# Two mixers: two panel splits moved ahead of the sums and merges in front of them, the branch gates' halves in another order, one dense group ahead of weighted values

## The reference

```python
h = rms_norm(x) * gain + shift                    # modulated by c through w_ada
q, kc, vc, ks, vs, kw, vw, g, mq, mk, mv, branch = split(h @ w_in)
a = nsa_mixer(...)     # compressed, selected and windowed attention, 8 heads, summed by gates
b = moba_mixer(...)    # 8 more heads
gates = sigmoid(branch)                           # two halves of 1024 columns
x = x + gate * ((gates_0 * (a @ w_up_nsa) + gates_1 * (b @ w_up_moba)) @ w_out)
x = x + gate * swiglu(...)                        # the layer's feed-forward part
```

## Time and profile before

| | |
|---|---|
| median of 3 runs | 2084.69 us (2081.43 to 2087.8) |
| the profiled execution | 2091.63 us, its span 2089.8 us |
| busy: PE, PE weight loads | 2009.8 us (96%), 1782.1 us (85%) |
| busy: DVE, ACT, POOL | 1465.0 us (70%), 1090.4 us (52%), 25.7 us (1%) |
| read from HBM | 369.15 MB, 177 GB/s over the span |
| granted PE clock, mean over the span | 0.98 of full |

### The profile page before, as it was taken

How to read it: one execution, slowest core, us unless ns; L and a number is a source line. 1 busy time by engine, 2 the same in 40 slices (tenths; PEclk the granted TensorE clock), 3 DMA queues, 4 the chain that set the end, 5 groups by cost and what they waited for, 6 DMA issues and landing times. The chain is left out here.

```text
span 2089.8 us, 31990 instructions
## 1 busy us (share of the span) xinstructions
PE 2009.8 (96%) x12846; PEld 1782.1 (85%) x12846; DVE 1465.0 (70%) x2323; ACT 1090.4 (52%) x1728; POOL 25.7 (1%) x46
## 2 busy tenths in 40 slices
PE   7899899999899899999999998999999999999999
PEld 4779898888789888899889777898898889898888
DVE  6777678877777577647766767677667757767774
ACT  3545544534545455535554655655545546855552
POOL 1001000000001000000000000000000000000000
PEclk9999999999999999999999999999999999999999
DMA  9445448876445357555556432455555554244554
GB/s 316 160 171 198 159 156 279 276 247 215 140 168 187 110 187 230 189 182 182 189 184 208 145 101 101 141 183 183 185 188 190 181 182 152 73 142 142 181 179 144
DMA packets 266211, 372.28 MB, mean 178 GB/s; under 512 B 8400, under 2 KB 160336, under 8 KB 266064
## 3 DMA queue, kind: packets, MB, share of 16 engines
q1 hardware_dynamic: 264736, 368.97, 53.0%
q10 hardware_dynamic: 1328, 1.26, 0.2%
HBM read 369.15 MB, written 1.05 MB: 177 GB/s over the span
## 5 line engine op out<-in xcount | busy, mean ns | idle before, releaser
L2222 DVE TENSOR_TENSOR parts<-ring,parts 128x2048 fp32r<-128x2048 f32 (+2 forms) x304 | 675.5, 2223 | 376.9 <-ACT parts L703 376.4
L703 ACT ACTIVATE parts<-ring 128x2048 fp32r<-128x2048 f32 (+2 forms) x304 | 565.6, 1861 | 592.8 <-PE psum L1470 323.7
L1470 PE MATMUL psum<-h,parts 128*128 128x512 f32 x1920 | 675.1, 396 | 0.0
L1468 PE MATMUL psum<-h,parts 128*128 128x256 f32 x1920 | 539.7, 281 | 2.9 <-DVE parts L2222 2.9
L1470 PEld LDWEIGHTS psum<-h,parts 128*128 128x128 f32 x1920 | 360.3, 188 | 85.9
L1468 PEld LDWEIGHTS psum<-h,parts 128*128 128x128 f32 x1920 | 362.8, 189 | 4.0 <-DVE parts L2222 3.9
L1462 PE MATMUL psum<-h,parts 128*128 128x256 f32 (+1 forms) x2088 | 265.6, 286 | 4.0 <-DVE h L2231 2.0
L1462 PEld LDWEIGHTS psum<-h,parts 128*128 128x128 f32 (+1 forms) x2088 | 255.3, 192 | 6.3 <-issue 3.6
L1462 PE MATMUL psum<-parts,h 128*128 128x512 f32 (+1 forms) x864 | 212.7, 400 | 19.1 <-DVE parts L2222 17.9
L1462 PEld LDWEIGHTS psum<-parts,h 128*128 128x128 f32 x864 | 161.3, 197 | 53.8 <-issue 17.4
L1470 PE MATMUL psum<-hid_hl,parts 128*128 128x512 f32 x528 | 188.2, 400 | 0.0
(11 more groups left out here) (255 smaller groups left out, 2118.4 us busy)
## 6 DMA issues: line engine op xcount, KB each, us to landing
ring<-in_w_ada SPq DMA_DIRECT2D x48, 1024.0 KB, 5.4
ring<-in_w_ffn_in SPq DMA_DIRECT2D x88, 512.0 KB, 4.8
ring<-in_ffn_w_gate SPq DMA_DIRECT2D x88, 512.0 KB, 3.7
ring<-in_ffn_w_up SPq DMA_DIRECT2D x88, 512.0 KB, 4.7
ring<-in_w_in SPq DMA_DIRECT2D x36, 1024.0 KB, 4.9
ring<-in_ffn_w_down SPq DMA_DIRECT2D x32, 1024.0 KB, 5.0
ring<-in_w_ffn_out SPq DMA_DIRECT2D x16, 1024.0 KB, 5.0
ring<-in_ffn_w_down SPq DMA_DIRECT2D x16, 768.0 KB, 4.4
```

What stands on the lines that cost most here:

```text
L703: act.activation(out, in_, func, **kw).then_inc(*sig(name, *keys))
L1468: pe.matmul(bank[:, 0:S], wt_hl[1], act[:, 0, :], start=start, stop=False, skip_group_check=True)
L1470: return pe.matmul(bank.rearrange("p (a s) -> p a s", a=2), wt_hl[0], act, start=False, stop=stop, skip_group_check=True)
L2222: dve.tensor_tensor(out, a, b, op).then_inc(*sig(name, *keys))
```

## The change

Four edits, all in the first stack's mixers (both layers). DVE makes the split of panel `("win", l, 4, 0)` before the head sums of group 3 and not behind head 0's mask and the `kcn` work. DVE makes the split of `w_up_moba`'s second panel before the first merged sum. ACT takes the in-place sigmoid of gate half 0 after the evacuations of `gbr` jobs 6 and 7. In iteration 23 PE takes one dense unit (24 matmuls of the last `gbr` panel) before weighted values 20, and one after.

```diff
@@ ACT, beside()
                             if n == 1 and k == 3 and i == 3:
                                 act.wait_ge(*at(("copied", ("gbr", l, 5))))
-                                run(br_gates[:, 0], br_gates[:, 0], ACT.Sigmoid, "act_gates",
-                                    ("gates", l, 0))
                                 run(br_gates[:, 1, 0:4], br_gates[:, 1, 0:4], ACT.Sigmoid,
                                     "act_step")
                                 for q in (6, 7):
...
                                         ("free", job), *([("gates", l, 1)] if q == 7 else []))
+                                run(br_gates[:, 0], br_gates[:, 0], ACT.Sigmoid, "act_gates",
+                                    ("gates", l, 0))
                                 act.preload_act_table_set(EXP_LN)
@@ PE, attention loop
                     if LAG <= i < HEADS + LAG:
                         turn(i - LAG)
+                    if i == 23:
+                        next(more, None)
                     if i > LAG:
                         weighted(i - LAG - 1)
-                    for _ in range(UNITS):
+                    for _ in range(UNITS - (i == 23)):
                         next(more, None)
@@ DVE, first_block()
                 for i in ORDER:
-                    if i < 3:
-                        splits.until((("win", l), i, 1), 2)
+                    splits.until((("win", l), i, 1), 2 if i < 3 else 1)
                     ks = [head_sums(n, HD) for t in range(TT) for _, _, n, _ in per[i]]
@@ DVE, behind the loop
                 y_lo(("tr y", l, 1, 1), 6, y_mix)
+                splits.until((("w_up_moba", l), 0, 0), 1)
 
                 dve.wait_ge(*at(("gates", l, 1)))
```

## The result

The changed kernel took 2066.07 us as the median of four runs (2065.3 to 2070.45), the kernel before 2084.78 us. The ratio is 0.9907, 95% interval 0.9889 to 0.9926: 19.4 us faster by the ratio (15 to 23), 18.7 us by the medians. Forecast were 22.3 us and 2062.4 us, range 2054 to 2072.

What follows compares the result with a forecast made beforehand. PE, busy nearly the whole span, bounds the kernel, so only its idle or low-clock time can be won. 14.4 + 1.7 + 6.2 = 22.3 us off the 2084.7 us median gives 2062.4 us, range 2054 to 2072.

Steps and rivals of the forecast that it cites:

- Part 1: Attention loop's start: splitting (win, l, 4, 0) before group 3's head sums brings compressed scores 7.4 and 7.0 us sooner, 14.4 us.
- rival (a): Short new waits at the loop's start and in wout keep the clock low; gain only 14 us, 2070 us; chance 0.10.
- The slow first twelve matmuls: On panel (win, l, 4, 0) after PE's idle time: full clock wins 2.31 us in layer 0, 1.86 in layer 1.
- Parts 2 and 3: Gate halves and dense unit near head 20: 0.7 us in layer 1 plus 1.0 in layer 0, 1.7 us.
- the row with 0.68 us: DVE's next gate products waited only 0.68 us for PE, so layer 1 can carry at most about 0.7 us forward.
- Part 4: Splitting w_up_moba's second panel before the merges: 3.1 us a layer, 6.2 us in all, with a new 1.8 us wait in wout.
- half a drop of the clock: Charge of 0.7 us a layer for slow matmuls behind the new 1.8 us wait in wout, lowering 3.8 to 3.1.
- (b): DVE and ACT some 4 us late at the first heads; gain 14 us or less, 2071 us or more; chance 0.07.
- (d): No change: time won in the mixers is paid back at the next load or norm-chain wait; 2085 us; chance 0.03.
- (e): Slower: moved splits wait for late hi parts and delay DVE's sums; 2 x 5 us lost, 2095 us; chance 0.02.
- Rival (c): Part 4's 1.8 us wait absent or costing no clock, sigmoid half worth 1.8; 26 us or more, 2058 us; chance 0.10.
- the wait for `y_mix`: Sign for the dense unit: PE's 1.98 us wait before weighted values 20 in layer 0 falls under 0.5 us.

Runs made afterwards that it cites:

- e_warm: Kernel before, no split moved, with 46 matmuls on zeros in PE's 5.9 us wait at each attention loop's start; ratio 0.9985, 3.1 us faster.
- e_fill: Changed kernel with four matmuls on zeros ahead of each eight of the 32 narrow matmuls of the compressed scores; ratio 0.9965 to the kernel before.
- e_gates: Kernel before with only the in-place sigmoid of gate half 0 moved behind the evacuations; ratio 0.9998, 0.4 us faster.
- e_again: The changed kernel measured again without further edits, giving its second trace; ratio 0.9912 to the kernel before, 18.4 us faster.
- e_sums: Kernel before with only the split of (win, l, 4, 0) moved ahead of group 3's head sums; ratio 0.9949, 10.6 us faster.
- e_merge: Kernel before with only the split of w_up_moba's second panel moved ahead of the first merged sum; ratio 0.9983, 3.5 us faster.
- e_lo2: Changed kernel with wout's second-half first low part before the last merged sum and ACT's next hi split before its last merged copy; ratio 0.9904 to the kernel before.

## Why the prediction was right, and where its terms were off

**Part 1** was forecast at 14.4 us. Its place gave 7.93 and 7.44 us (forecast 7.4 and 7.0). The wait for ACT's copy was 0.23 and 0.30 us; the sum had allowed 0.75 (107.0 - 106.25), though rival (a) spoke of 0.5. The slow first twelve matmuls were rightly counted as lost to idle time: e_warm shows it, with 2.36 and 1.91 us against 2.31 and 1.86. What was missing is behind it. In layer 0, from the compressed scores to the last scores, all seven traces with part 1 (without e_fill) take 112.3 to 112.4 us, and the five without it 109.2 to 110.9; the low stretch there is 6.8 us long and was 3.4 or absent. That takes back 1.7 us. In layer 1 the traces do not divide that way: 110.6 to 110.8 us in four of the seven with part 1 and 112.2 to 112.5 in the other three, 109.2 to 110.8 in three of the five without it and 112.4 to 112.5 in two. e_warm, with full clock at the loop's start and no split moved, has the short stretch in layer 0 (110.93) and the long one in layer 1 (112.39), so the missing earlier drop alone does not explain it. The reason is open. Up to the last scores part 1 kept 6.21 us in layer 0 and 7.35 in layer 1 (19.89 + 110.65 - 12.45 - 110.74), 13.6 us together.

**Parts 2 and 3** were forecast at 1.7 us, and this step failed, in layer 1. I took from the row with 0.68 us that DVE's products bound what could be carried on. I missed ACT's copy of the turned probabilities of head 22, which stands behind the same sigmoids, table load and split and which PE met just in time. In the changed kernel PE waits 1.52 us for it. Layer 1's place, from the last scores to the second panel of `w_up_nsa`, took 16.25 us before, 16.23 in e_gates and 16.26 in e_again: it gave nothing where 0.7 was forecast. In the first trace of the change it took 17.77, because the clock was low behind the 1.52 us wait (4.59 us for 24 matmuls instead of 3.07). That loss is no mark of the change: three kernels without parts 2 and 3 (e_sums, e_merge, e_warm) took 17.79 to 17.81 there, with the clock low behind the old 2.21 us wait. In layer 0 the place gave 0.84 (forecast 1.0). That the slow clock there falls inside the wait for ACT was right: in e_warm it did not fall, the `aux` wait grew to 2.33 us, and the place took 19.44 us, as before.

**Part 4** was forecast at 3.1 us a layer with half a drop of the clock. It gave 3.62 in layer 0, without one, and 2.11 in layer 1 with one: 5.7 instead of 6.2. The new wait was 2.24 us, not 1.8, because PE came sooner: its 96 matmuls start 11.40 us before `wout` (688.72 to 700.12), 5.70 for each 48, where I had counted the listed 5.90, which overlaps with what follows. The chain of merges ended where it was worked out to end. e_lo2 shows that the order of merges and splits is what PE waits for there; it moved one operation on DVE and one split on ACT, and which of them did it was not tried. To set the price of the clock the prediction called 1.8 us a wait between 1.98 and 2.21; it is shorter than both, so the half that it charged had no row on its lower side.

The sum by these measures is 13.6 - 0.7 + 5.7 = 18.6 us, where -0.7 is 0.84 in layer 0 less the 1.52 by which layer 1's place took longer. **Rival (a)**, the clock that does not come back, came for a part in the first trace: of four places where short waits were left, two (layer 1) lost it and layer 0's loop got a longer low stretch, worth about 1.5, 1.5 and 1.7 us. Only half a drop a layer was charged for this in part 4 and none in the others. That is the larger part of the 3.7 us missing to 22.3 in this trace.

The Trainium skill's "TensorE: Matmul & The Clock Gate" ("A second HAM failure mode: psum-queue depth-cycling") says that frequent short idles make the clock fall and rise. The first trace agrees where 1.52 and 2.24 us of waiting were followed by 0.63 and 0.64 of clock, and disagrees at layer 0's 1.97 and 2.25 us waits, which were not. The second trace of the same kernel has the same four waits and lost the clock behind none. Over all kept traces that have these waits, the clock was low behind the 1.52 us wait in two of five, behind layer 0's 1.97 in two of six, and behind the 2.24 to 2.25 us wait in four of six in layer 1 and in none of six in layer 0. So a short wait may cost the clock, and what decides it is not shown.

**Rivals (b), (d) and (e)** did not come: DVE's masks did not hold PE at the loop's start, no load held PE up there, and both moved splits ended before what they stood in front of. **Rival (c)** failed by the same chain as parts 2 and 3; its other half, a wait in `wout` that costs no clock, came in the second trace. Of the signs named in the prediction one was missed by a little: the wait for `y_mix` is 0.56 us and not under 0.5.

## What to carry to other kernels

A split or copy whose input is ready early but that stands in an in-order queue behind a wait can cost the consumer a wait, and here cost the clock behind it too; ask which engine idles at that moment, and move it there. Moving one member of a chain whose total is fixed (sigmoids, table load, split, copies) only moves the wait: follow the whole queue up to the next thing that the consumer needs before counting a gain. When the long wait is gone, the order of the small operations behind it sets the next one.

## What the runs showed of the hardware that was not expected

The same instructions between the compressed scores and the last scores took 109.2, 110.5 to 110.9 or 112.2 to 112.5 us in different traces, by how long the low clock lasted there (not at all, 3.4 or 6.8 us). These differences are as large as one of the smaller parts of this change, and they are one reason why parts 2, 3 and 4 can hardly be told from nothing by the total. The same wait of 1.5 us, in the same kernel, was followed by a low clock in one trace and not in another. Filling a wait of 5.9 us with 5.2 us of matmuls on zeros kept the clock at 1.00, while 16 such matmuls among the 32 narrow ones did not prevent the drop that follows those.
